# Three extra weight buffers for eight weight slots read directly, and the middle of a gated convolution worked on GpSimd, in a two-block transformer kernel

## What is computed

```python
h = rms_norm(x, norm1_w[l])
cols = split_cols(h @ w_in[l], IN_SIZES)
a_b, a_c, a_u = cols[0:3]          # each 512 x 256

def short_conv_mixer(b_gate, c_gate, u, conv_w, conv_b):
    v = c_gate * u
    y = lax.conv_general_dilated(v, conv_w[:, None, :].astype(v.dtype), ...)  # width 3, causal, per channel
    return b_gate * (y + conv_b)

def compress_tokens(kv, cmp_idx, pos, w1, w2):
    B = kv.shape[0]
    blocks = kv[:, cmp_idx] + pos
    hdn = jax.nn.silu(blocks.reshape(B, blocks.shape[1], -1) @ w1)
    return hdn @ w2
```

## Time and profile before

| what | value |
|---|---|
| time, median of 3 runs | 1951.4 us (1950.84 to 1953.42) |
| time of the profiled execution | 1951.64 us |
| its span on the core | 1949.9 us |
| TensorE busy | 1858.1 us (95%) |
| VectorE busy | 880.9 us (45%) |
| GpSimd busy | 989.2 us (51%) |
| ScalarE busy | 427.3 us (22%) |
| mean granted TensorE clock | 0.97 |

### The profile page before, as it was taken

The page is one execution under the profiler, slowest core; times in us unless marked ns, Lnnn a source line. Parts: engine busy times, 40 slices in busy tenths (PEclk is TensorE's granted clock), DMA queues, the critical chain, the costliest instruction groups (busy, mean ns, idle before and its releaser), DMA issues.

```text
span 1949.9 us, 21942 instructions
## 1 busy us (share of the span) xinstructions
PE 1858.1 (95%) x8480; PEld 1451.6 (74%) x8480; DVE 880.9 (45%) x1372; ACT 427.3 (22%) x911; POOL 989.2 (51%) x568
## 2 busy tenths in 40 slices
PE   7898889999999998999999999999999899999996
PEld 5685556788888886777887778777778668888885
DVE  5317764564026322435004365665654654404434
ACT  3114564121012101222003132455400210000001
POOL 3441110566666665455664444444466646666664
PEclk9899899999999999999999889999999899999998
DMA  4530010222222222122322111311122212222221
GB/s 158 175 109 26 24 44 22 87 97 97 97 97 95 97 89 107 67 76 76 105 97 76 59 61 63 121 66 66 55 97 93 80 55 97 98 97 97 98 97 54
DMA packets 47735, 164.50 MB, mean 84 GB/s; under 512 B 5504, under 2 KB 6720, under 8 KB 47249
## 3 DMA queue, kind: packets, MB, share of 16 engines
q1 hardware_dynamic: 44240, 156.62, 23.0%
q10 hardware_dynamic: 3393, 6.48, 1.2%
HBM read 160.10 MB, written 2.12 MB: 83 GB/s over the span
## 4 chain that ended last, share of the span: by engine, by line
PE 84%; DVE 8%; ACT 3%; issue 2%; POOL 2%; DMA 1%; SPq 0%; DVEq 0%; ACTq 0%; POOLq 0%
PE bank L666 83%; DMA w_raw<-in_w 1%; POOL w_lo_t L1976 1%; PE bank L934 1%; DVE tmp L1457 1%; DVE o_hi L1435 1%; DVE o_lo L1436 1%; POOL w_hi_t L1974 0%; DVE att_l_t L1759 0%; ACT L1091 0%; DVE att_l_t L1900 0%; ACT rstd_t L1137 0%; DVE tmp L1879 0%; ACT sq L1124 0%; DVE g_st L1931 0%
## 5 line engine op out<-in xcount | busy, mean ns | idle before, releaser
L1974 POOL TENSOR_SCALAR w_hi_t<-w_raw 128x1024 fp32r<-128x1024 f32 x276 | 296.5, 1074 | 913.4 <-PE bank L666 844.7
L1976 POOL TENSOR_TENSOR w_lo_t<-w_raw,w_hi_t 128x1024 fp32r<-128x1024 f32 x276 | 674.5, 2444 | 23.1
L666 PE MATMUL bank<-h_hi,w_hi_t 128*128 128x512 f32 x1344 | 548.0, 408 | 35.1 <-POOL w_lo_t L1976 23.5
L666 PE MATMUL bank<-h_lo,w_hi_t 128*128 128x512 f32 x1344 | 531.1, 395 | 1.3 <-DVE h_lo L1517 1.3
L666 PE MATMUL bank<-h_hi,w_lo_t 128*128 128x512 f32 x1344 | 530.2, 395 | 0.0
L666 PEld LDWEIGHTS bank<-h_hi,w_hi_t 128*128 128x128 f32 x1344 | 256.7, 191 | 112.7 <-issue 43.7
L666 PEld LDWEIGHTS bank<-h_lo,w_hi_t 128*128 128x128 f32 x1344 | 257.1, 191 | 57.4 <-DVE h_lo L1517 3.5
L666 PEld LDWEIGHTS bank<-h_hi,w_lo_t 128*128 128x128 f32 x1344 | 256.6, 191 | 55.5 <-issue 0.5
L666 PE MATMUL bank<-hid_hi,w_lo_t 128*128 128x512 f32 x432 | 168.1, 389 | 0.0
L666 PE MATMUL bank<-hid_hi,w_hi_t 128*128 128x512 f32 x432 | 168.0, 389 | 0.0
L666 PE MATMUL bank<-hid_lo,w_hi_t 128*128 128x512 f32 x432 | 168.0, 389 | 0.0
(11 more groups left out here) (264 smaller groups left out, 2260.1 us busy)
## 6 DMA issues: line engine op xcount, KB each, us to landing
w_raw<-in_w SPq DMA_DIRECT2D x284, 512.0 KB, 3.2
x_sb<-in_x SPq DMA_DIRECT2D x4, 512.0 KB, 7.3
x_sb<-in_x ACTq DMA_DIRECT2D x2, 1024.0 KB, 5.6
alibi<-in_alibi SPq DMA_DIRECT2D x8, 256.0 KB, 5.1
out_y<-x_sb SPq DMA_DIRECT2D x8, 256.0 KB, 2.0
toep<-table ACTq DMA_DIRECT2D x4, 256.0 KB
decay<-in_decay SPq DMA_DIRECT2D x1, 1024.0 KB, 4.8
wqb<-in_wqb ACTq DMA_DIRECT2D x1, 384.0 KB, 4.9
```

Source lines behind the costliest of these rows:

```text
L666: return pe.matmul(out, lhs, rhs, start=start, stop=stop, **kw)
L1974: pool.tensor_scalar(hi, raw, 1.0, 0.0, ALU.mult, ALU.add).then_inc(*did("w_hi", i))
L1976: pool.tensor_tensor(lo, raw, hi.bitcast(F32), ALU.subtract).then_inc(*did("w_lo", i))
```

## The change

The eight direct slots get three buffers of their own (`u_raw`): two are parts of `y` that are not in use yet (y[:, 0:2] and y[:, 2:4], written first by the convolution and by the nsa attention), the third takes room that was left empty. The ring `w_raw` now holds split slots only, slot number n of the 276 in buffer n % 3. SyncE still issues everything in one order; a direct slot waits for TensorE's step three direct slots back, a split slot for `w_lo` three split slots back.

VectorE keeps one product for each layer of the convolution: ac times r_h, au times that, and ab times the finished convolution, now straight into `y`. What is between the last two becomes seven instructions on GpSimd for each chunk, with a wait behind nearly each. They stand in GpSimd's list ahead of the split of slot 27 (chunk 0) and of slot 30 (chunk 1), and begin by waiting until VectorE has taken au out of its bank. VectorE waits for the last of them ahead of ab's product.

```diff
@@ TensorE, cmp_up
-                pe.wait_ge(C.sem[f"w_landed{i % RAW}"], 16 * (i // RAW + 1))
+                u = WHOLE.index(i)
+                pe.wait_ge(C.sem[f"u_landed{u % NW}"], 16 * (u // NW + 1))
...
@@ VectorE, layers ac, au, ab
-                        chain(dve.tensor_tensor(conv_t[:, 1, 2:2 + T], ps(name)[:], r_h[:], ALU.mult))
-                        ins = dve.tensor_tensor(conv_t[:, 1, 2:2 + T], conv_t[:, 1, 2:2 + T], r_h[:], ALU.mult)
+                        ins = dve.tensor_tensor(conv_t[:, 1, 2:2 + T], ps(name)[:], r_h[:], ALU.mult)
                     elif key == "au":
                         ins = dve.tensor_tensor(v, ps(name)[:], conv_t[:, 1, 2:2 + T], ALU.mult)
                     else:
-                        yc = y[:, c]
-                        w = [col("conv_w", 2 * k + c) for k in range(3)]
-                        chain(dve.tensor_scalar(yc, conv_t[:, 0, 2:2 + T], w[2], col("conv_b", c), ALU.mult, ALU.add))
-                        for k in (1, 0):
-                            chain(dve.scalar_tensor_tensor(out=yc, in0=conv_t[:, 0, k:k + T], scalar=w[k], in1=yc,
-                                                           op0=ALU.mult, op1=ALU.add))
-                        chain(dve.tensor_tensor(yc, yc, r_h[:], ALU.mult))
-                        ins = dve.tensor_tensor(conv_t[:, 1, 2:2 + T], ps(name)[:], yc, ALU.mult)
+                        own("conv_y", c)
+                        ins = dve.tensor_tensor(y[:, c], ps(name)[:], conv_t[:, 1, 2:2 + T], ALU.mult)
                     ins.then_inc(*release(name))
                     dve.wait_ge(*evacuated(name))
-                    if key == "ab":
-                        dve.tensor_copy(y[:, c], conv_t[:, 1, 2:2 + T]).then_inc(*did("conv_v", c))
-                        own("conv_v", c)
...
@@ GpSimd
+        def conv(c):
+            pool.wait_ge(*evacuated(("au", c)))
+            v, yc, t = conv_t[:, 0, 2:2 + T], conv_t[:, 1, 2:2 + T], y[:, c]
+            w = [col("conv_w", 2 * k + c) for k in range(3)]
+            pool.tensor_tensor(v, v, r_h[:], ALU.mult).then_inc(*did("p_conv", c, 0))
+            pool.wait_ge(*after("p_conv", c, 0))
+            pool.tensor_scalar(yc, v, w[2], col("conv_b", c), ALU.mult, ALU.add).then_inc(*did("p_conv", c, 1))
+            for k in (1, 0):
+                pool.tensor_scalar(t, conv_t[:, 0, k:k + T], w[k], None, ALU.mult).then_inc(*did("p_conv", c, 2, k))
+                pool.wait_ge(*after("p_conv", c, 2, k))
+                pool.tensor_tensor(yc, yc, t, ALU.add).then_inc(*did("p_conv", c, 3, k))
+                pool.wait_ge(*after("p_conv", c, 3, k))
+            pool.tensor_tensor(yc, yc, r_h[:], ALU.mult).then_inc(*did("conv_y", c))
+
         for n, i in enumerate(SPLIT):
...
+            if i in (SLOTS[("ab", 0)][0] + 2, SLOTS[("ab", 1)][0] + 2):
+                conv(1 if i > SLOTS[("ab", 1)][0] else 0)
...
@@ SyncE
+                    if i in WHOLE:
+                        u = WHOLE.index(i)
+                        if u >= NW:
+                            sp.wait_ge(*slot_done[WHOLE[u - NW]])
+                        sp.dma_start(u_raw[u % NW], a["w"][i]).then_inc(C.sem[f"u_landed{u % NW}"], 16)
+                        continue
+                    n = SPLIT.index(i)
                     if n >= RAW:
-                        sp.wait_ge(*(slot_done[n - RAW] if n - RAW in WHOLE else after("w_lo", n - RAW)))
+                        sp.wait_ge(*after("w_lo", SPLIT[n - RAW]))
```

More of the change, by code:

```diff
@@ L286 @@
 RING = {i: n % SPL for n, i in enumerate(SPLIT)}
+NW = 3
 UNNORMED = ("n1",)
@@ L336, in _program @@
         C.sem[f"w_landed{s}"] = ctx.enter_context(nc.semaphore(f"w_landed{s}"))
+    for s in range(NW):
+        C.sem[f"u_landed{s}"] = ctx.enter_context(nc.semaphore(f"u_landed{s}"))
     for c in range(8):
@@ L552, in _program @@
     for g in range(4):
-        srcs = ([("ev", "conv_v", c) for c in range(2)] if g == 0 else
+        srcs = ([ev(("ab", c)) for c in range(2)] if g == 0 else
                 [ev(({1: "nsa_o", 2: "mla_o"}[g], c) if g < 3 else ("sb_o", c)) for c in range(2)])
@@ L849, in _ @@
                     wsl = slice((j % 4) * 256, (j % 4) * 256 + 256)
-                    last = mm(ps(("cmp_u", kv))[:, 0:256], cmp_x[:, c0:c0 + P], w_raw[:, i % RAW, wsl], j == 0, j == 15)
+                    last = mm(ps(("cmp_u", kv))[:, 0:256], cmp_x[:, c0:c0 + P], u_raw[u % NW][:, wsl], j == 0, j == 15)
                 if s == 3:
```

16 lines of the change are left out of this document (8 added, 8 removed).

## The result

The changed kernel takes 1932.08 us (median of 4 runs, 1927.78 to 1933.11) beside 1951.12 us for the kernel before on the same chip (4 runs, 1950.68 to 1953.42): a ratio of 0.9896, 95% interval 0.9879 to 0.9913, 19 us less by the medians. The profiled execution took 1933.11 us, against the 1951.64 us of before: 18.5 us less. The forecast was 1935.6 us with 15.9 us less. The total came out well inside the range, but of its two terms one was too large and the other less than a third of what was measured.

The account below looks back on a forecast made before the run. TensorE, busy 1558.8 of 1607 us behind 343 us, bounds the kernel, so the gain must arise ahead of that. Buffers -11.9 and convolution -4.0 make -15.9 us: 1935.6 us, own span 1932 to 1939, range 1930 to 1945.

Parts of the forecast that it names:

- its two terms: Ahead of 343 us: the buffers, -11.9 us, and the convolution leaving VectorE, -4.0 us.
- Part 1, the waits for slots 9, 13 and 15: From 41 to 110 us: own direct buffers remove TensorE's waits for these loads and splits, 11.9 us.
- the five terms: Slot 9: wait 3.06, low clock 1.7; slot 13: 0.74; slot 15: wait 3.84, low clock 2.6 us.
- Part 1, what comes late next: Direct stretch: the norm of cq comes late next, its squares about 1 us ahead; loss up to 3 us.
- Loads in the first 20 us: At the start: three direct slots load behind x in the same queue, costed at 0 to +1.5 us.
- Part 2, GpSimd's instructions: Convolution: seven instructions a chunk, 4 x 1.43 + 3 x 1.87 = 11.3 us; two-column product 1.4 to 2.5.
- Part 2, the hold-up of VectorE: Behind au 0: SBUF-to-SBUF operations meeting a running GpSimd instruction wait for its end, 5.6 us delay by 191 us.
- rival E: Convolution: GpSimd's whole 22.6 us delay VectorE and TensorE, and the clock halves behind each; 1957.6 us, chance 0.03.
- rival A: Convolution: held-up VectorE costs more than was taken off it, +2 in place of -4; 1941.6 us, chance 0.23.
- Part 2, the clock: From 150 to 310 us: TensorE's waits at ab 0 and ab 1 counted, 3.74 and 3.34 us, without clock term.
- Rival C: GpSimd's instructions slip between VectorE's, clock stays up through nsa attention: -12 and -8, 1931.5 us; chance 0.1.
- Part 2, by chunks: Convolution: ac 0 -2.0, chunk 0 -0.5, ac 1 0, chunk 1 -1.5 us; together -4.0, bounds -9 to +5.

Follow-up runs that it names:

- the next two: Second and third profiles of the unchanged changed kernel (e0 and e11); e0 measured 1931.18 us, e11 was run for the profile alone.
- e8: Changed kernel with GpSimd's one-column products written as multiplication plus addition of 0.0, in the convolution and residual sums: 1936.23 us, ratio 0.9929.
- e3: Changed kernel with the convolution's middle worked on VectorE right behind au's product, GpSimd code left out: 1942.4 us, ratio 0.9953.
- e10: The kernel before, unchanged, run once more for one more profile; no total time is given.
- e0: The changed kernel again, unchanged, for a second trace and more runs: 1931.18 us, ratio 0.9886.
- e11: The changed kernel a third time, unchanged, for one more profile; direct stretch 59.46 us, no total time given.
- e6: Changed kernel with six more one-column products in GpSimd's chain of chunk 0: 1935.25 us, ratio 0.9917.

## Why the prediction was right, and where it was not

- **What bounds the kernel, and where the gain would lie.** Right. All of the gain arose ahead of slot 32. "The rest of the span keeps its length within 1 us" held for the first profile (0.7 us) and not for the next two (3.4 and 3.9 us); the reason is not in the change's own stretches but far behind, in which of two waits the clock falls behind.
- **Part 1, the waits for slots 9, 13 and 15.** The mechanism was right and each of the five terms went: the clock is 1.00 from 60 to 100 us and at 92 to 96 us, no transfer is in the chain, and TensorE is busy 39.8 of 40 us. With the split held the stretch gives 11.4 to 12.05 us, the 11.9 of the sum. In the change itself it gives 7.7 to 9.9 us. The product of v1 comes 6.3 us earlier in the first profile and 8.8 to 9.7 us in the next two, where "some 12 us" had been named as a sign.
- **Part 1, what comes late next.** This step failed. The prediction looked at the norm of cq and allowed up to 3 us of loss, outside the sum. It was the square of nq0, one layer earlier, and the reason was not a queue of loads but GpSimd: slots 7 and 9, loaded early, are split while VectorE works from SBUF to SBUF. The prediction had the earlier trace rows for exactly this effect, used them for the convolution, and did not apply them to the splits that its own Part 1 moved to the front. A new wait ahead of 110 us was one of its own signs of being wrong, and 1.95 us of it are there. The loss was 2 to 4 us, the upper end where the clock fell behind the wait. The norm of cq became a wait too, of 0.2 to 0.5 us in two of the three profiles.
- **Loads in the first 20 us.** Costed at 0 to +1.5 us. The first direct step comes 1.5, 0.2 and 0.3 us later in the three profiles; the 1.5 goes with the moment of full rate, 3.2 us later there than before, which differs by execution.
- **Part 2, GpSimd's instructions.** 11.3 us a chunk forecast, 9.7 and 9.6 us measured: 1.1 to 1.6 us for sums and products of two tensors, 1.56 to 1.73 for the one-column product, and 0.76 for the one with two columns, below the lower bound of 1.4. The Trainium skill, "GPSIMD Engine Reference", section 4.1 (Engine selection), has one input "roughly line-rate". The trace nearly agrees for the form with a multiplication and an addition (0.76 us beside VectorE's 0.55) and does not for the multiplication alone; the experiment e8 shows that the form makes the difference.
- **Part 2, the hold-up of VectorE.** This step failed as well. 5.6 us forecast for chunk 0, 1.4 us measured as busy time, 0.2 us in the part from au 0 to ab 0. "Each one that meets a running GpSimd instruction waits for its end" was taken from one meeting with a split's subtraction. It holds for that one and for the sum of two tensors at 172.66 us, but not for one-column products, 3.2 of the chain's 9.7 us, beside which VectorE's operations take 0 to 0.3 us longer. So the rule of the Trainium skill that the prediction names beside rival E ("SBUF — State Buffer", "two separate sides": the one blocks the other for a whole instruction) agrees with the subtraction and not with these products. The sign named for it, operations of 1.5 us and more beside the chain, did not come: the longest takes 1.27 us. This is the term that rival A had made larger still.
- **Part 2, the clock.** The forecast counted only waits here: 3.74 us and 3.34 us. But the earlier trace rows had a granted clock of 0.83 at 160 to 180 us, and it was 0.80 from ac 1 to au 1. After the change it is 0.96 to 1.00 up to au 1, worth 7.9 us of TensorE's busy time in this pair. It isn't VectorE's load as such: e3 keeps the chain on VectorE and has 1.00 from ab 0 to au 1 as well. It is single waits, gone (ab 0) or shorter (ac 1), and the clock behind them. The same step had been done in Part 1 for slots 9 and 15 (4.3 of the 11.9 us) and was left out here. Rival C had it, at a chance of 0.1.
- **Part 2, by chunks.** The terms were -2.0 for ac 0, -0.5 for chunk 0, 0 for ac 1 and -1.5 for chunk 1. In the first profile ac 0 gave -3.4 us, chunk 0 gave -5.3 (+0.2 ahead of ab 0, -5.5 behind it), ac 1 gave -4.2 and what is behind au 1 -0.2. So chunk 0 was too small because a hold-up that did not come was set against the wait at ab 0. And ac 1, put at nothing because "the 0.69 us are given back to the split", turned a wait of 1.92 us into one of 1.44 us and kept the clock up; against e10 it gave -1.9 us. Behind au 1 it was -0.2 us in the first profile and -1.7 in e0 and e11. The 3.34 us of the earlier trace rows did go, but the next wait took their place:

```profile
264.07 2.90 PE L670 MATMUL bank<-mk,mq 96*128 96x384 f32 x4 [4.46 <-ACT att_pt L1347]
```

  TensorE's waits for L1347 between ac 0 and slot 32 grew from 5.9 us (longest 2.4) to 8.2 us (longest 4.5). The estimate of 1.5 us for ab 1 had looked at GpSimd's chain and not at the attention tile behind it.
- **VectorE's wait for conv_y.** Forecast short or nil, and it is not among its waits. Chunk 1's chain ends at 248.2 us, and VectorE takes ab 1 out of its bank at 251.24 us, after a wait for TensorE and not for GpSimd.

The first profile's sum by the forecast's own terms is then -7.7 + 1.5 for the buffers in place of -11.9, -13.1 for the convolution in place of -4.0, and +0.7 behind. Two errors of opposite sign, +5.7 and -9.1 us, left a total 2.7 us off. That the total came out so near is luck; alone it would have passed for a confirmation of both parts.

## What to carry to other kernels

Where a load is made earlier, ask what the engine that consumes it will now run beside, and cost that with the rows that show the two engines together. Where TensorE's granted clock is below 1.00 behind a wait and the change shortens that wait, cost the clock's share with it, even where the work taken off ahead of it is as small as 0.69 us. The other engine's time counts only with what it holds up: look for it instruction by instruction, since here a sum of two tensors held VectorE and a product with one column hardly did, and look where its next long instruction will fall. To tell the load from the place, put marks on both sides of each piece of work. Read the total against marks along the span, since two wrong terms can add up to a right total.

## What the runs showed of the hardware that was not expected

- On GpSimd a product with a column (128x512) in the one-operation form takes 1.56 to 1.88 us, and with a second operation, even the addition of 0.0, 0.72 to 1.01 us.
- Six such one-operation products, back to back on GpSimd for 10.43 us (e6), made VectorE's SBUF-to-SBUF operations beside them 0.3 us longer at most (0.87 in place of 0.55 us), while a split's subtraction beside the same kind of operation made it 1.6 to 1.9 us longer.
- Behind the same wait of 1.95 us in the direct stretch TensorE's granted clock fell in three profiles (0.57 to 0.64 from 52 to 56 us) and stayed at 1.00 in four.
- Behind the same wait of 1.6 us, about 1126 us into the changed kernel, TensorE's granted clock fell in some executions (0.63 on average over the next 16 us) and stayed at 1.00 in others of the same kernel. Where it stayed up, a second wait came 36 us on and the clock fell behind that, and the kernel was 3 us longer, not shorter.
- The moment at which TensorE first reaches full rate was between 14.9 and 18.3 us over thirteen profiles, with the same kernel at 18.28, 16.01 and 16.66 us.
